# Reordered evacuations in a fused encoder block: softmax sums behind the bank reads, head copies on ScalarE, squares on GpSimd, and a weight ring that waits for x

## What is computed

```
h = rmsnorm(x) * norm_g ;  z = h @ w_in, split into q_a(512) kv_a(256) k_pe(64) gate_a(2048)
    conv_b conv_c conv_x gate_c (1024 each)  merge_a merge_c (2048 each)
q = rmsnorm(q_a) @ w_uq  -> 16 heads of 128 + 64 rotary ; kv = rmsnorm(kv_a) @ w_ukv -> k_nope 128, v 128
k = [k_nope, k_pe] ; q, k = rmsnorm per head ; rotary on the last 64
A  = softmax(q k^T / sqrt(192)) v, all keys ;  Cv = conv_b * conv3(conv_c * conv_x)
ya = (A * silu(gate_a)) @ w_branch_attn ;  yc = (Cv * silu(gate_c)) @ w_branch_conv
x  = x + (sigmoid(merge_a) * ya + sigmoid(merge_c) * yc) @ w_out
x  = x + sigmoid(rmsnorm(x) @ w_ple_gate) * (p @ w_ple_proj)
```

## Time and profile before

| | |
|---|---|
| median of 3 runs | 1649.59 us (1648.67 to 1651.38) |
| profiled execution | 1646.86 us |
| its span on the slowest core | 1645.3 us (eight cores: 1637.1 to 1645.3) |
| PE busy | 1515.8 us, 92% |
| PEld, DVE, ACT, POOL busy | 674.3 (41%), 866.5 (53%), 661.8 (40%), 216.7 us (13%) |
| chain that ended last | PE 71%, DVE 9%, ACT 7%, issue 7%, DMA 4% |
| mean granted TensorE clock of the core | 0.987 |

### The profile page before, as it was taken

The page is one execution under the profiler, slowest core; times in us unless marked ns, Lnnn a source line. Parts: engine busy times, 40 slices in busy tenths (PEclk is TensorE's granted clock), DMA queues, the critical chain, the costliest instruction groups (busy, mean ns, idle before and its releaser), DMA issues.

```text
span 1645.3 us, 22556 instructions; the slowest of 8 cores (1637.1 to 1645.3 us)
## 1 busy us (share of the span) xinstructions
PE 1515.8 (92%) x7858; PEld 674.3 (41%) x7858; DVE 866.5 (53%) x1056; ACT 661.8 (40%) x868; POOL 216.7 (13%) x230
## 2 busy tenths in 40 slices
PE   4597978899898998989899899999999999999998
PEld 1243433434343443434334343444444444444443
DVE  4475444677676877787767876111111111344455
ACT  4435645565555566656556664110111101112211
POOL 0000000131211213122121213100100010100000
PEclk9899999999999999999999999999999999999999
DMA  8635533332222333232233222734543543984652
GB/s 261 189 94 111 158 52 61 64 66 51 56 51 50 60 65 60 60 67 53 54 66 67 48 49 46 122 59 76 90 72 63 90 83 63 211 205 79 122 122 77
DMA packets 51710, 143.67 MB, mean 87 GB/s; under 512 B 7568, under 2 KB 7696, under 8 KB 51472
## 3 DMA queue, kind: packets, MB, share of 16 engines
q0 software_dynamic: 23328, 78.13, 28.6%
q1 hardware_dynamic: 28272, 64.11, 12.9%
HBM read 189.39 MB, written 8.39 MB: 120 GB/s over the span
## 4 chain that ended last, share of the span: by engine, by line
PE 71%; DVE 9%; ACT 7%; issue 7%; DMA 4%; SPq 1%; DVEq 0%; ACTq 0%
PE ps L264 70%; DVE acc L278 2%; PE ps L263 2%; DMA xo_82<-x_own 1%; DMA xo_75<-x_own 1%; DMA fb<-f_235 1%; ACT eb_187 L267 1%; SPq L258 1%; ACT eb_186 L267 1%; ACT P_225 L267 1%; ACT P_226 L267 1%; DVE q_237 L284 1%; DVE zb L284 1%; ACT f_235 L267 1%; ACT P_227 L267 1%
## 5 line engine op out<-in xcount | busy, mean ns | idle before, releaser
L278 DVE TENSOR_TENSOR acc<-acc,P_225 128x1024 f32<-128x1024 f32 x75 | 102.2, 1362 | 34.8 <-ACT P_225 L267 33.9
L278 DVE TENSOR_TENSOR acc<-acc,P_227 128x1024 f32<-128x1024 f32 x75 | 100.1, 1335 | 35.0 <-ACT P_227 L267 33.6
L278 DVE TENSOR_TENSOR acc<-acc,P_226 128x1024 f32<-128x1024 f32 x74 | 97.5, 1318 | 31.8 <-ACT P_226 L267 30.6
L264 PE MATMUL ps<-Qn_222,Kn_218 128*128 128x512 bf16 x256 | 77.1, 383 | 0.0
L264 PE MATMUL ps<-Qn_221,Kn_217 128*128 128x512 bf16 x256 | 76.6, 381 | 0.0
L270 DVE SCALAR_TENSOR_TENSOR mt_274<-mt_270,ps 128x512 f32<-128x512 f32 x16 | 11.0, 687 | 119.6 <-PE ps L264 107.2
L270 DVE SCALAR_TENSOR_TENSOR mt_275<-mt_271,ps 128x512 f32<-128x512 f32 x16 | 11.0, 687 | 113.6 <-PE ps L264 113.6
L267 ACT ACTIVATE mt_269<-ps 128x512 f32<-128x512 f32 x16 | 9.6, 597 | 124.8 <-PE ps L264 124.8
L267 ACT ACTIVATE mt_268<-ps 128x512 f32<-128x512 f32 x16 | 9.6, 597 | 121.7 <-PE ps L264 121.7
L267 ACT ACTIVATE P_225<-ps,sk_54 128x1024 bf16<-128x1024 f32 x43 | 47.9, 1114 | 24.8 <-PE ps L264 23.3
L267 ACT ACTIVATE P_225<-ps,sk_55 128x1024 bf16<-128x1024 f32 x43 | 47.9, 1113 | 20.9 <-PE ps L264 15.5
(11 more groups left out here) (1641 smaller groups left out, 4027.7 us busy)
## 6 DMA issues: line engine op xcount, KB each, us to landing
fb<-f_235 SPq DMA_DIRECT2D x128, 128.0 KB, 2.3
ring_129<-w_tiles POOLq DMA_DIRECT2D x25, 512.0 KB, 5.6
ring_130<-w_tiles POOLq DMA_DIRECT2D x24, 512.0 KB, 6.0
ring_132<-w_tiles POOLq DMA_DIRECT2D x24, 512.0 KB, 5.4
ring_131<-w_tiles POOLq DMA_DIRECT2D x22, 512.0 KB, 5.7
ringm_276<-w_tiles POOLq DMA_DIRECT2D x11, 512.0 KB, 6.0
ringm_277<-w_tiles POOLq DMA_DIRECT2D x11, 512.0 KB, 6.6
ringm_278<-w_tiles POOLq DMA_DIRECT2D x11, 512.0 KB, 6.5
```

The source lines that it names most:

```text
L264: return P.op("pe", lambda h: h.matmul(bank_ap, lhsT=lhsT, rhs=rhs, start=start, stop=stop), reads=reads, writes=writes)
L278: return P.op("dve", lambda h: h.tensor_tensor(out=out, in0=in0, in1=in1, op=op), reads=reads, writes=writes)
```

## The change

- `cols` gets one more column, ln of EPS (`C_LNE`). ScalarE copies one element at the very start. `x_stat` no longer writes `epso`; one Exp on ScalarE makes it from the Ln in `rsto`. The third `x_stat` stands one `kv_own` later.
- The first four ring loads additionally wait for the cast of `wlk[1]`.
- `hold` marks banks 0 to 5 as just used.
- The first four conv groups alternate between banks 6 and 5.
- `parts` and the second list have another order, and a number of gate matmuls of their own for each step.
- `up_pieces(0)` goes through banks 7, 0, 1, 2, 3, 4.
- Per head, q0's two copies go from VectorE to ScalarE, their squares from ScalarE to GpSimd, and two V copies from VectorE to ScalarE.
- In a round the order of calls becomes: scores, piece, scores and exps, conv step, lsum or fin, softmax sum, the step after the piece, product with V. Pieces start in round 1 of a head; lsum is in round 0, fin in round 3; the rotary sum (`rot`) and Qn (`qfin`) come one and two pieces later in the list.

```diff
+        act(colx.ap[:, 3:4], ones.ap[:, 0:1], AF.Copy, [ones], [colx])
         cast_wlq(0)
...
         def hold(v):
+            tick[0] += 1
             for i in range(6):
                 held[i] = v
+                lastuse[i] = tick[0]
...
-            ring.add_slot(at(RING0 + i * 4096, BF16, 2048, f"ring{i}"))
+            ring.add_slot(at(RING0 + i * 4096, BF16, 2048, f"ring{i}"), deps=[wlk[1].res.w])
...
-            n = 342 if i < 2 else 340
-            ts(epso.ap[:, i * 342:i * 342 + n], bk.ap[:, 0:n], EPS / D, EPS * EPS, MUL, ADD, [bk], [epso])
...
         kv_own(2)
+        kv_own(3)
         x_stat(2)
+        act(epso.ap, rsto.ap[:, 0:T], AF.Exp, [rsto, cols], [epso], bias=col(C_LNE))
         act(rsto.ap, rsto.ap, AF.Exp, [rsto], [rsto], scale=-0.5)
-        for kc in range(3, 16):
+        for kc in range(4, 16):
...
-            bk = banks[6]
+            bk = banks[conv_banks.pop(0) if conv_banks else 6]
...
+        conv_banks = [6, 5, 6, 5]
...
+        parts = [(6, L(q_sq, 0, 0)), (6, L(q_sq, 0, 1)), (6, L(q_sq, 1, 0)), (6, L(q_ss, 0)), (6, L(q_sq, 1, 1)), (6, L(kv_sq, 0)), (6, L(q_ss, 1)), (6, L(kv_sq, 1)),
+                 (6, L(kpe_mul, 0, rsto)), (6, L(kv_ss, 0, 1024, epso)), (6, L(kv_ss, 1, 1536, epso)), (6, L(factors, 2048)), (6, L(kpe_ss, 0)), (6, L(kpe_mul, 1, rsto)),
+                 (8, L(q_out, 0)), (8, L(q_out, 1)), (8, L(kpe_ss, 1)), (8, L(q_out, 2)), (8, L(q_out, 3)), (8, L(kpe_dup, 0)), (8, L(kv_out, 0, 1024)), (8, L(kpe_dup, 1)), (8, L(kv_out, 1, 1536))]
+        for n, fn in parts:
+            fill(n)
             fn()
+            if fn is parts[11][1]:
                 use_tanh[0] = True
+        fill(10)
...
+        for n, fn in [(8, L(kv_sq, 2)), (8, L(r_stat, 0)), (8, L(kv_sq, 3)), (8, L(r_stat, 1)), (8, r_eps), (2, r_factor), (8, L(kv_ss, 2, 0, epsr)), (8, L(kv_ss, 3, 512, epsr)),
+                      (4, L(kpe_mul, 2, rstr)), (4, L(factors, 1024)), (12, L(kpe_ss, 2)), (4, L(kpe_dup, 2)), (4, L(kpe_mul, 3, rstr)), (8, L(kv_out, 2, 0)), (8, L(kv_out, 3, 512)),
+                      (8, L(kpe_ss, 3)), (4, L(kpe_dup, 3))]:
+            fill(n)
             fn()
...
-                vcopy(q0.ap[:, sl], bk.ap, [bk], [q0])
-                act(qsq[qb].ap, q0.ap[:, sl], AF.Square, [q0], [qsq[qb]])
+                P.op("act", lambda h: h.copy(out=q0.ap[:, sl], in_=bk.ap), reads=[bk], writes=[q0])
+                ptt(qsq[qb].ap, q0.ap[:, sl], q0.ap[:, sl], MUL, [q0], [qsq[qb]])
...
-                if r % 2 == 0:
-                    P.op("act", lambda h: h.copy(out=V_.ap[:, r * 512:(r + 1) * 512], in_=bk.ap), reads=[bk], writes=[V_])
-                else:
-                    vcopy(V_.ap[:, r * 512:(r + 1) * 512], bk.ap, [bk], [V_])
+                P.op("act", lambda h: h.copy(out=V_.ap[:, r * 512:(r + 1) * 512], in_=bk.ap), reads=[bk], writes=[V_])
...
+            return [(pc(qrope), None), (pc(qnope, 0), None), (pc(qnope, 1), None), (pc(kup, 0), rot), (pc(qss), None), (pc(kup, 1), None),
+                    (pc(kup, 2), None), (pc(kup, 3), None), (pc(vup, 0), qfin), (pc(kss), None), (pc(vup, 1), None), (pc(vup, 2), None), (pc(vup, 3), None)]
...
+            fn(banks[(7, 0, 1, 2, 3, 4)[i % 6]])
...
-                emit_acc(g)
-                fn, after = pieces.pop(0) if pieces else (None, None)
+                fn, after = pieces.pop(0) if pieces and kt > 0 else (None, None)
                 if fn:
                     fn(bU)
...
+                quantum()
+                if kt == 0 and lsum:
+                    lsum(bU)
+                if kt == 3 and fin:
+                    fin()
+                emit_acc(g)
                 if after:
                     after()
-                quantum()
                 emit_PV(g)
```

More of the change, by code:

```diff
@@ L21 @@
 C_GA, C_CB, C_CC, C_CX, C_GC, C_MA, C_MC = 832, 2880, 3904, 4928, 5952, 6976, 9024
-C_NG, C_PG, C_GQL, C_GKV, C_GQN, C_GQR, C_GQP, C_GKN, C_GKC, C_SGN, C_INVF, C_PHT, C_PH, C_EPS, C_LNS, C_CW, C_CB_ = (
-    0, 16, 32, 36, 38, 39, 40, 41, 42, 43, 45, 46, 47, 48, 49, 50, 74)
-NCOL = 82
+C_NG, C_PG, C_GQL, C_GKV, C_GQN, C_GQR, C_GQP, C_GKN, C_GKC, C_SGN, C_INVF, C_PHT, C_PH, C_EPS, C_LNS, C_CW, C_CB_, C_LNE = (
+    0, 16, 32, 36, 38, 39, 40, 41, 42, 43, 45, 46, 47, 48, 49, 50, 74, 82)
+NCOL = 83
 MAGIC = 12582912.0
@@ L424, in __init__, with add_slot, pump @@
                 self.q = []
-            def add_slot(self, b):
+            def add_slot(self, b, deps=()):
                 self.free.append(b)
-                self.pump()
-            def pump(self):
+                self.pump(deps)
+            def pump(self, deps=()):
                 while self.free and self.nxt < len(self.src):
@@ L434, in pump @@
                     self.nxt += 1
-                    ld("pool", b, src, out_ap=b.ap[:, 0:n])
+                    ld("pool", b, src, out_ap=b.ap[:, 0:n], deps=deps)
                     self.q.append(b)
@@ L701, in L @@
             return lambda: fn(*a)
[L703 to L707, removed]
+        parts = [(6, L(q_sq, 0, 0)), (6, L(q_sq, 0, 1)), (6, L(q_sq, 1, 0)), (6, L(q_ss, 0)), (6, L(q_sq, 1, 1)), (6, L(kv_sq, 0)), (6, L(q_ss, 1)), (6, L(kv_sq, 1)),
[3 more added lines that the diff above has]
+            fill(n)
             fn()
-            if fn is parts[13]:
+            if fn is parts[11][1]:
                 use_tanh[0] = True
+        fill(10)
         for i, b_ in enumerate((cosQ, sinQ)):
@@ L765, in r_factor @@
             act(rstr.ap, rstr.ap, AF.Exp, [rstr], [rstr], scale=-0.5)
-        for fn in [L(kv_sq, 2), L(r_stat, 0), L(kv_sq, 3), L(r_stat, 1), r_eps, L(kv_ss, 2, 0, epsr), L(kv_ss, 3, 512, epsr), r_factor, L(factors, 1024),
-                   L(kpe_mul, 2, rstr), L(kv_out, 2, 0), L(kv_out, 3, 512), L(kpe_ss, 2), L(kpe_dup, 2), L(kpe_mul, 3, rstr), lambda: None, lambda: None, L(kpe_ss, 3), L(kpe_dup, 3)]:
-            fill(8)
+        for n, fn in [(8, L(kv_sq, 2)), (8, L(r_stat, 0)), (8, L(kv_sq, 3)), (8, L(r_stat, 1)), (8, r_eps), (2, r_factor), (8, L(kv_ss, 2, 0, epsr)), (8, L(kv_ss, 3, 512, epsr)),
+                      (4, L(kpe_mul, 2, rstr)), (4, L(factors, 1024)), (12, L(kpe_ss, 2)), (4, L(kpe_dup, 2)), (4, L(kpe_mul, 3, rstr)), (8, L(kv_out, 2, 0)), (8, L(kv_out, 3, 512)),
+                      (8, L(kpe_ss, 3)), (4, L(kpe_dup, 3))]:
+            fill(n)
             fn()
@@ L899, in fin @@
                 ptt(AT[h].ap, Osb.ap, fb.ap, MUL, [Osb, fb], [AT[h]])
-            return [(lsum, None), (None, fin)]
+            return lsum, fin
         def emit_nope(g, start):
@@ L938, in build_nc @@
         fill(1 << 20)
-        for fn, after in up_pieces(0):
-            fn(bU)
+        for i, (fn, after) in enumerate(up_pieces(0)):
+            fn(banks[(7, 0, 1, 2, 3, 4)[i % 6]])
             quantum()
@@ L951, in build_nc @@
                 ld("pool", wup[h % 2], wup_d[h + 2])
-            pieces = (tail_pieces(h - 1) if h > 0 else []) + (up_pieces(h + 1) if h + 1 < NH else [])
+            pieces = up_pieces(h + 1) if h + 1 < NH else []
+            lsum, fin = tail_pieces(h - 1) if h > 0 else (None, None)
             for kt in range(16):
@@ L993, in build_nc @@
                 if blk == 0:
-                    tails[0][0](banks[7])
-                    tails[1][1]()
+                    tails[0](banks[7])
+                    tails[1]()
                 for kc in range(16):
@@ L1159, in _host_inputs @@
     cols[:, C_EPS] = EPS
+    cols[:, C_LNE] = math.log(EPS)
     cols[:, C_LNS] = -0.5 * math.log(192.0)
```

2 lines of the change are left out of this document (removed).

## The result

The changed kernel takes **1606.07 us** (median of 1605.93, 1606.07 and 1607.19), the kernel before 1649.13 beside it: a ratio of 0.9738, with a 95% interval of 0.9719 to 0.9757. That is 43 us faster, where 63 were forecast: inside the range of 1565 to 1620, above the likeliest case's own 1570 to 1604.

What follows compares the result with a forecast made beforehand. The prediction took TensorE, with idle gaps, as the bound. Attention 38, the stages from 105 to 288 us 16 and the first 105 us 9 sum to 63 us off 1646.86, with 2.73 to the median: 1587 us, range 1565 to 1620.

Steps and rivals of the forecast that it cites:

- The first 105 us: Start of the kernel: holding ring tiles frees x's DMA stream, 8 us, plus 1 for an earlier hT: 9 us gained.
- Rival B: Start of the kernel: ring tiles go ahead of wlk loads, casts and hT slip; head gains 1, 1595 us; chance 0.10.
- 105 to 288 us: Gates and latent statistics: of 25.9 us idle 11 stay, 15 gained plus 1 for the clock: 16 us.
- the 38 us: Attention: 20 of 58 us of TensorE waits stay, 38 gained, minus 3 new, plus 3 of clock: 38 us.
- (3): Attention: q0's two squares per head go to GpSimd; 3 us cost in all, bounds nothing to 53 us.
- (4): Attention: lsum, fin and the rotary steps shift by a round or two; priced within the 3 us of (3).
- minus 3 new: Attention: the 3 us of new cost allowed for (3) and (4) together.
- (2): Attention: q0's two copies per head and two V copies go to ScalarE; q0's 14.4 us wait becomes 2.
- rival C: Attention: the rotary sum on GpSimd makes VectorE stand before Qr, slowing the kernel to 1677 us; chance 0.06.
- The lock that I feared: Attention: GpSimd and VectorE take turns on SBUF, so squares could take up to 3.5 us per head from VectorE.
- A: Attention gains only 10: ScalarE's queue holds reads behind an exp, the lock takes VectorE time; 1615 us; chance 0.17.
- D: Attention: queue order is not what makes readers late, so it gains only 3; 1622 us; chance 0.05.

Runs made afterwards that it cites:

- head_only: The kernel before with only the changes of the first 105 us (early ScalarE copy, held ring loads, epso on ScalarE, later third x_stat); 1635.6 us, ratio 0.9878.
- no_ringwait: The changed kernel with the ring loads no longer held for the wlk[1] cast; 1612.65 us, ratio 0.9786.
- order_only: The kernel before with only the new order of the attention round and pieces, no moves between engines; 1626.9 us, ratio 0.9830.
- best1: sq_act_split with the rotary sum on VectorE and pieces starting in round 2 of a head; 1590.94 us, ratio 0.9651.
- best2: sq_act_split with the rotary sum on VectorE, pieces from round 3, lsum in round 1, fin in round 4, Qn later; 1587.02 us, ratio 0.9617.
- sq_act_split: The changed kernel with q0's squares back on ScalarE, q0 as two tiles and Kn as four; 1593.8 us, ratio 0.9660.
- sq_act: The changed kernel with only q0's squares moved back from GpSimd to ScalarE; 1592.40 us, ratio 0.9663.
- split: The changed kernel with q0 as two tiles and Kn as four, squares still on GpSimd; 1597.69 us, ratio 0.9688.
- old_engines: The changed kernel with q0's copies, its squares and half the V copies back on their old engines; 1601.55 us, ratio 0.9715.

## Why the prediction was right and wrong

**The first 105 us: right, for the reasons given.** 9 forecast, 12 measured. The last part came 10 us earlier than before (8 forecast); head_only shows 11 us for the part alone, no_ringwait 6.6 for the hold alone. The idle time fell by 8.5 us; the other 3.5 are TensorE's busy time (65.4 to 61.9), the clock of 0.98 for 0.93, which I had priced in the other stages and forgot here. Rival B's mechanism is there and small: the last cast ends at 71.5, rsto was ready at 69.8, so the casts hold hT up by 1.6 us, which the prediction had named as a sign of being wrong. The three last wlk loads took 10.3 us from the first one's issue (60.70) to the last cast's start (70.96), far from the 3.7 of the SP queue by itself. That is near the 11 that the packet-by-packet turn of the Trainium skill gave (DMA: Bandwidth & Descriptors, Queues, rings and completion order). Held ring tiles are not free to whoever loads next.

**105 to 288 us: right.** 16 forecast, 14 measured. The 7.4 us kv wait and the 5.3 of kval are gone; of the 11 us that I let stay, 12.3 stayed, though not the same ones: the kpe sums now wait 6.2 us for ScalarE's squares of k_pe, one of them behind factors, where the lists were shifted rather than mended. The 1 us for the clock came to 0.4 (mean 0.95 for 0.96).

**Attention: the 38 us were mis-sized, in steps (3) and (4) above all.** The stage was to be under 700 us and took 708. In the stage of the table TensorE's idle time fell from 58.8 to 43.6. By owner:

| reader | before | after |
|---|---|---|
| q0 copies | 14.6 | 0 |
| ub, zb | 15.1 | 8.3 |
| V copies | 7.7 | 1.8 |
| t_238 | 2.6 | 0 |
| K copies | 3.9 | 9.2 |
| f and acc | 1.2 | 9.2 |
| ccb (conv copies on ScalarE) | 1.8 | 3.3 |
| t1b, skt, P | 11.6 | 11.8 |

The first four rows give back 29.9 us, of 38 forecast; t1b, skt and P, which were to halve with the other small groups, stayed. The next three rows are 14.8 us of new waits, against "minus 3 new". And the clock gave 1.0 us of TensorE's busy time (664.8 to 663.8), where 3 were counted. So of the 23 us that are missing some 8 are gains that did not come, 12 new waits, 2 the clock.

What failed is step (4) first, "I price that within the 3 us". order_only, which has neither (2) nor (3), has all the new waits already: K copies 9.5 us, f and acc 9.4, ccb 4.0. best1 shows that f comes of pieces in round 1 (it starts them in round 2), best2, which also moves lsum by a round, that acc comes of lsum in round 0; best2 is 6.8 us faster than sq_act_split (the rotary sum on VectorE, the later pieces and the later Qn are in it too). The moved `rot` belongs to (4) as well, see rival C.

Step (3) failed too: by sq_act the squares cost 13.7 us, where they had a share in the 3. How these are made up isn't shown. q0's wait by whole tile is in them; split's 8.4 us can't be put down to it, since split frees the K copies as well.

Step (2) came out right in its number, q0's 14.4 to about nothing, and by luck: the move of the copies had little to do with it, since order_only has 1.6 without it.

Why did I miss it? I asked what GpSimd's square delays *downstream*, its reader qss, two rounds later: well covered. I did not ask what waits for the square to be *done reading*: the next write to q0. Before, such a wait did no harm: the earlier trace rows show VectorE idle for 0.9 us in all ahead of the 30 copies. And I took Kn's 2.9 us as fixed and priced q0 by it; in the new order it rose to 8.4.

**The lock that I feared takes little from VectorE in sum, but what it takes falls in a bad place.** By the rule of the Trainium skill (SBUF — State Buffer, Who interferes with whom) GpSimd's squares could have taken up to 3.5 us a head from VectorE. The two kernels that differ in the squares alone, the changed one and sq_act, run the same 542 VectorE instructions of the stage in 498.6 and 496.2 us: 2.4 us in all, not 53. The sum hides a shift, however. In the changed kernel 63 K squares took 42.8 us, in sq_act 33.6, in old_engines 30.9; the softmax sums got shorter instead (mean 1316 ns, 1353 in sq_act). The second instance above shows how: AT, which GpSimd comes to only behind both squares, runs beside the first K square, which takes 2.36 us, where the next one takes 0.42. A K square stands ahead of bank reads in VectorE's queue, and the next K copy waits for it. GpSimd pays as well: its square takes 1.03 us at the least and 1.86 in the first instance, and that is what ScalarE waits for.

**The rivals.** A came nearest in size (attention 10, where 15 was measured) and is half right: ScalarE's queue does hold the reads, but behind waits for GpSimd and VectorE, not behind an exp, and the lock took little of VectorE's time. C's mechanism came, at a smaller price than C's and not by the squares: VectorE stands 22.1 us before Qr in 14 waits, and 20.6 in 13 both in order_only and in sq_act, which have no squares on GpSimd; the moved `rot` makes it, as Qr now comes one round behind the rotary sum and not two. TensorE does stand behind it, another of the prediction's signs of being wrong: of the 17.9 us that end behind such a Qr, some 14 at most are the stand's, by an estimate that counts 1.58 us for each. What taking it away is worth isn't shown: best1, with the rotary sum on VectorE, starts the pieces later as well, and its stage is 706.8 us where sq_act_split has 707.3. D is refuted by order_only.

**What is left open:** how the squares' 13.7 us divide among q0's tile, the longer K squares and GpSimd's queue, and why TensorE's granted clock is lower with the moves. The table's idle time and stage show less than 13.7 us between the changed kernel and sq_act (3.9 and 9.1) for two reasons. The profiled execution of sq_act is the longest of its four, 10.5 us under that of the changed kernel. And its slowest core lacks matmul records (3975 for 4065). From the first score matmul to the first merge activation the median of eight cores is 708.4 us and 697.4, and on the six cores with all records the waits there are 43.1 to 43.6 us and 35.5 to 36.0: 11 us, of which some 8 are waits.

## What to carry to other kernels

When an operation moves to a slower engine, price it from both ends: who reads its result, and who waits to overwrite its *input*. Where dependencies are tracked by tile, a tile that is filled in pieces by one engine and read in pieces by another ties them into lockstep; splitting the tiles of q0 and K costs nothing and gave 8 us here. And before moving copies between engines, try the order of the queue by itself: it held all that attention gained, the three moves together added nothing, because one of them took what another gave. And where two engines get in each other's way, look at single instructions: VectorE's busy time hardly moved, while the instructions that others wait for got longer.

## What the runs showed that I had not expected

- A GpSimd product of 128x512 has no one price: the same square ran in 1.04 us at 551.64, where VectorE stood idle, and in up to 2.10 us elsewhere (1.86 beside VectorE's sum in the first instance), mean 1.67 of 16 in the group of the first halves:

```profile
L281 POOL TENSOR_TENSOR qsq_232<-q_237 128x512 bf16<-128x512 f32 x16 | 26.7, 1669 | 133.2 <-ACT q_237 L835 124.8
```

- The rotary sum on GpSimd got faster by being moved later, 1264 ns for 1742 to 1774, which fits that VectorE now mostly stands still before Qr while it runs.
